# Sample tokens of a product-key expert layer by gathered rows, 384 dense tokens, and gate products in half steps

## The reference, cut to what matters

```python
q = (xb @ w_pq).reshape(..., 8 heads, 2, 128)
s = einsum('thpd,phnd->thpn', q, sub_keys)          # 128 keys per half
s1, i1 = top_k(s[:, :, 0], 16); s2, i2 = top_k(s[:, :, 1], 16)
top, pos = top_k(s1[..., :, None] + s2[..., None, :], 16)
eidx = (i1 * 128 + i2) at pos                       # 16 experts per head
gate = softmax(top)
a = einsum('thkd,td->thk', u_tab[eidx], xb)
out = einsum('thk,thkd->td', gelu(a) * gate, v_tab[eidx])
```

## Time and profile before

| | |
|---|---|
| median of 3 runs | 1866.88 us (1865.66 to 1868.56) |
| profiled execution | 1866.18 us |
| its span | 1864.5 us |
| TensorE busy | 1780.4 us (95%) |
| VectorE / ScalarE / GpSimd busy | 63% / 39% / 58% |
| DMA | 442.39 MB, mean 237 GB/s |
| mean granted TensorE clock | 0.978 |

### The profile page before, as it was taken

The page is one execution under the profiler, slowest core; times in us unless marked ns, Lnnn a source line. Parts: engine busy times, 40 slices in busy tenths (PEclk is TensorE's granted clock), DMA queues, the critical chain, the costliest instruction groups (busy, mean ns, idle before and its releaser), DMA issues.

```text
span 1864.5 us, 27254 instructions
## 1 busy us (share of the span) xinstructions
PE 1780.4 (95%) x10594; PEld 1698.5 (91%) x10594; DVE 1183.9 (63%) x2350; ACT 728.1 (39%) x983; POOL 1083.0 (58%) x612
## 2 busy tenths in 40 slices
PE   7899999799999999999999998999999999999995
PEld 3899887688999999999999998989999999999995
DVE  3441343627898799985666665446677777777746
ACT  2454232323333333354554544443444444444431
POOL 1667221132337788854554454477877888887851
PEclk9899999899999999999999999999999999999997
DMA  8545121233215888868687786799999999999951
GB/s 273 172 148 170 62 97 57 75 113 103 91 51 163 273 275 281 275 211 276 233 269 242 250 260 217 228 400 369 363 353 357 377 350 377 353 368 361 364 185 48
DMA packets 191200, 442.39 MB, mean 237 GB/s; under 512 B 20064, under 2 KB 106080, under 8 KB 190816
## 3 DMA queue, kind: packets, MB, share of 16 engines
q1 hardware_dynamic: 82320, 251.88, 39.5%
q0 software_dynamic: 36864, 134.23, 19.4%
q10 hardware_dynamic: 71888, 54.53, 8.8%
HBM read 381.42 MB, written 59.17 MB: 236 GB/s over the span
## 4 chain that ended last, share of the span: by engine, by line
PE 87%; DVE 4%; DMA 3%; ACTq 2%; ACT 2%; issue 1%; POOL 1%; SPq 0%; DVEq 0%; POOLq 0%
PE ps L866 57%; PE ps L652 17%; PE ps L876 5%; ACTq L1136 2%; PE ps L672 2%; PE ps L681 1%; DMA gelu_scratch<-ga 1%; PE ps L841 1%; ACT stage L1143 1%; DMA tab<-in_tab 1%; DMA raw<-in_w 1%; ACT tHi L1092 1%; PE ps L764 0%; DMA ug<-in_urows,eidx 0%; PE ps L798 0%
## 5 line engine op out<-in xcount | busy, mean ns | idle before, releaser
L612 POOL TENSOR_TENSOR tLo<-tab,tHi 128x1024 fp32r<-128x1024 f32 x256 | 635.5, 2482 | 357.9 <-ACT tHi L1092 356.5
L1092 ACT CAST tHi<-tab 128x1024 fp32r<-128x1024 f32 x256 | 267.9, 1047 | 331.9 <-PE ps L866 321.1
L866 PE MATMUL ps<-actHi,tLo 128*128 128x416 f32 x1024 | 361.7, 353 | 5.5 <-issue 5.3
L866 PE MATMUL ps<-hHi,tLo 128*128 128x416 f32 x1024 | 364.5, 356 | 0.0
L866 PE MATMUL ps<-hLo,tHi 128*128 128x416 f32 x1024 | 361.6, 353 | 0.0
L866 PE MATMUL ps<-actHi,tHi 128*128 128x416 f32 x1024 | 359.6, 351 | 0.0
L866 PE MATMUL ps<-hHi,tHi 128*128 128x416 f32 x1024 | 358.8, 350 | 0.0
L866 PE MATMUL ps<-actLo,tHi 128*128 128x416 f32 x1024 | 357.4, 349 | 0.0
L600 POOL TENSOR_TENSOR wLo<-raw,wHi 128x1024 fp32r<-128x1024 f32 x53 | 127.7, 2409 | 316.0 <-ACT wHi L930 316.0
L866 PEld LDWEIGHTS ps<-actHi,tLo 128*128 128x128 f32 x1024 | 192.5, 188 | 7.6 <-issue 5.6
L866 PEld LDWEIGHTS ps<-hHi,tHi 128*128 128x128 f32 x1024 | 193.2, 189 | 2.8
(11 more groups left out here) (310 smaller groups left out, 2617.8 us busy)
## 6 DMA issues: line engine op xcount, KB each, us to landing
tab<-in_tab SPq DMA_DIRECT2D x256, 512.0 KB, 6.1
raw<-in_w SPq DMA_DIRECT2D x101, 512.0 KB, 3.9
gelu_scratch<-ga ACTq DMA_DIRECT2D x128, 208.0 KB, 4.4
gate_scratch<-stage ACTq DMA_DIRECT2D x13, 2048.0 KB, 14.1
gt<-gate_scratch SPq DMA_DIRECT2D x32, 832.0 KB, 5.8
gin<-gelu_scratch SPq DMA_DIRECT2D x128, 208.0 KB, 7.8
xT<-in_xT SPq DMA_DIRECT2D x1, 2176.0 KB, 10.0
out_y<-yo SPq DMA_DIRECT2D x8, 272.0 KB
```

Source lines behind the costliest of these rows:

```text
L612: pool.tensor_tensor(tLo[:, n % SPL], tab[:, n % TABS], tHi[:, n % SPL].bitcast(F32), ALU.subtract).then_inc(s_tlo, 1)
L866: last = mm(ps[:, bank, 0:TD], w, x[:, k, 0:TD], start=first, stop=end)
L1092: nc.scalar.copy(tHi[:, n % SPL], tab[:, n % TABS]).then_inc(s_thi, 1)
```

## The change

- The dense tokens are now 384 prompt tokens (TD = 384); the sparse tile holds the last 128 prompt tokens.
- The 32 sample tokens also go by gathered rows: a partition holds one token and one of four groups of two heads, so their 4096 picks are 32 items (PB) ahead of the 128 others. Items are NDOT = 160 per table, 320 in all, in place of 256. ScalarE repeats their query and their h four times (`q_b`, `h_b`); they have a retrieval of their own with two heads, run first; h is brought to rows twice, after chunk 3 for the samples and after chunk N_SHUF = 51 for the prompt. The four partial sums are added by a product with a folded identity after chunk 168.
- Dots: eight in each of the four tiles of level two, tile 0 among them; two with each of 48 gate steps; 32 after them, three per chunk; so that all dots are done ahead of the second pass. Row sums follow at 10 in 7 chunks.
- Gate steps begin at chunk 52 over 64 chunks. The products of a step go in two halves, over three PSUM banks (4, 5, 7), with a wait and a copy for each half.
- Three gelu buffers in place of two, one semaphore each.
- The picks' transposes, of three tiles in place of four, stand at chunk 51, and the sum over the samples is read at chunk 168.

The core of the diff:

```diff
-TD = T - P
-STILES = [TD, 0, 128, 256, TD - P]
+TD = T - P - TS
+STILES = [TD, 0, 128, 256]
...
-NIT = 2 * P
-L2_DOTS = 10
-N_SHUF = 56
-G_FIRST, G_SPAN = 57, 60
-N_GELU = NCH + 20
+PB = P * TS // P
+NDOT = P + PB
+NIT = 2 * NDOT
+L2_DOTS = 8
+N_SHUF = 51
+G_FIRST, G_SPAN = 52, 64
+N_GELU = NCH + 2
+GATE_BANKS = (4, 5, 7)
...
-    due = NIT - 152 + min(152, (n - NCH + 1) * 13 // 10)
-    return due if n > N_GELU else min(due, P)
+    if n < NCH:
+        return min(NDOT, PB + 2 * NSTEP + 3 * (n - G_FIRST - G_SPAN))
+    return NDOT + max(0, min(NDOT, (n - N_GELU) * 10 // 7))
 
 
 def item_time(q):
 
-    if q < 40:
-        return 14 + q
-    if q < 92:
-        return G_FIRST + (q - 40) * G_SPAN // NSTEP
-    if q < 104:
-        return 120 + (q - 92) * 2 // 3
-    return NCH + (q - 104) * 10 // 13
+    if q < PB:
+        return 12 + q
+    if q < PB + 2 * NSTEP:
+        return G_FIRST + (q - PB) // 2 * G_SPAN // NSTEP
+    if q < NDOT:
+        return G_FIRST + G_SPAN + (q - PB - 2 * NSTEP) // 3
+    return N_GELU + (q - NDOT) * 7 // 10
 
...
-        ga = at("ga", [P, 2, TD], SPL_AT + 24576)
+        ga = [at(f"ga{i}", [P, TD], (SPL_AT + 24576, SPL_AT + 24576 + 4 * TD, pos_sq + 6528)[i]) for i in range(3)]
...
             def gather(q):
 
                 if q == 0:
-                    pool.wait_ge(s_eidx, 1)
+                    pool.wait_ge(s_hr, 1)
+                if q == 0 or q == PB:
+                    pool.wait_ge(s_eidx, 1 if q == 0 else 2)
                 if q >= UG:
                     pool.wait_ge(s_item, q - UG + 1)
-                pool.indirect_dma_start(ug[:, q % UG, :], None, a["urows"] if q < P else a["vrows"],
-                                        bass.IndirectOffsetOnAxis(ap=eidx[:, q % P:q % P + 1], axis=0)).then_inc(s_ug[q % UG], 16)
+                pool.indirect_dma_start(ug[:, q % UG, :], None, a["urows"] if q < NDOT else a["vrows"],
+                                        bass.IndirectOffsetOnAxis(ap=eidx[:, q % NDOT:q % NDOT + 1], axis=0)).then_inc(s_ug[q % UG], 16)
...
-                if st:
-                    pe.wait_ge(s_gev, st)
-                for t in range(STEP_TOK):
-                    out = ps[:, 4 + t // 4, t % 4 * P:(t % 4 + 1) * P]
-                    last = mm(out, oh2[:, st % 2, t, :], w1[:, st % 2, t, :], start=True, stop=True)
-                last.then_inc(s_gmm, 1)
+                for part in range(2):
+                    i = 2 * st + part
+                    if i >= len(GATE_BANKS):
+                        pe.wait_ge(s_gev, i - len(GATE_BANKS) + 1)
+                    for t in range(4):
+                        last = mm(ps[:, GATE_BANKS[i % 3], t * P:(t + 1) * P], oh2[:, st % 2, 4 * part + t, :],
+                                  w1[:, st % 2, 4 * part + t, :], start=True, stop=True)
+                    last.then_inc(s_gmm, 1)
 
...
+                if n == 3:
+                    pe.wait_ge(s_idr, 1)
+                    pe.wait_ge(s_hb, 1)
+                    sparse_h((h_b[:, 0], h_b[:, 1]))
...
+                    pe.wait_ge(s_item, PB)
+                    sparse_h((hHi[:, :, TD:TP], hLo[:, :, TD:TP]))
...
+                    for part in range(2):
+                        i, t0 = 2 * st + part, STEP_TOK * j + 4 * part
+                        act.wait_ge(s_gmm, i + 1)
+                        f(stage[:, b % 2, :, t0:t0 + 4].rearrange("p c t -> p t c"),
+                          ps[:, GATE_BANKS[i % 3], :].rearrange("p (t c) -> p t c", c=P), ACT.Identity).then_inc(s_gev, 1)
...
+            where = [best_b[:, 1], best_b[:, 2]]
+            retrieve(2, m16_b[:], ix_b[:], best_b[:, 0], where, lambda part: None)
+            indices(eidx[:, 0:PB], where)
+            for i in range(NST):
+                where = [best[:, 1, i, :], best[:, 2, i, :]]
+                retrieve(PH, m16[:, i], ix[:, i], best[:, 0, i, :], where, lambda part: sparse(L2_DOTS * i + part))
                 if i == 0:
-                    stt(eidx[:], best[:, 1, 0, :], float(NKEY), best[:, 2, 0, :], ALU.mult, ALU.add).then_inc(s_eidx, 1)
...
-                sparse(4 * L2_DOTS + st + 1)
+                sparse(PB + 2 * (st + 1))
...
-            sparse(4 * L2_DOTS + NSTEP + 4)
-            v.wait_ge(s_gev, NSTEP)
+            sparse(sparse_until(NCH - GRP))
+            v.wait_ge(s_gev, 2 * NSTEP)
             for c in range(GRP):
                 act_32(c)
-                sparse(4 * L2_DOTS + NSTEP + 5 + c)
                 act_lo(c)
+                sparse(sparse_until(NCH - GRP + c))
+            sparse(NDOT)
```

More of the change, by code:

```diff
@@ L418, in build @@
         s_gelu = sem("gelu_ready")
[L419 removed]
+        s_gas = [sem(f"gelu_stored{i}") for i in range(3)]
         s_oh = sem("one_hots_ready")
@@ L851, in _, with sparse_h @@
             key_scores(HP - 1)
[L853 to L857, removed]
+            def sparse_h(parts):
+                for k in range(KT):
+                    for i in range(2):
+                        last = mm(h_rows[:, k * P:(k + 1) * P], parts[i][:, k], identR[:], start=(i == 0), stop=(i == 1))
+                last.then_inc(s_hr, 1)
             def product(n, hi_in, lo_in, bank):
@@ new lines, in _, with retrieve @@
+                if j % 8 == 7:
+                    for u in (j // 8 * 2, j // 8 * 2 + 1):
+                        last = top16([m16_b[:, u]], [ix_b[:, u]], [sc_b[:, u, :]])
+            link(last)
+            def retrieve(nh, m, x, top, where, some):
+                nk = nh * PK
+                rank = iota[:, 0:PK].unsqueeze(1).broadcast_to([P, nk, PK])
+                cand_, tcur_, pos_, pab_ = cand[:, 0:nh], tcur[:, 0:nh], pos16[:, 0:nk], pab[:, 0:nk]
+                pabf_, pcut_, ixf_ = pabf[:, :, 0:nk], pcut[:, 0:nk], ixf[:, 0:2 * nh]
+                nc.vector.tensor_copy(ixf_, x)
+                halves = m.rearrange("p (h two) k -> p h two k", two=2)
+                half = ixf_.rearrange("p (h two) k -> p h two k", two=2)
+                tt(cand_[:, :, 0:16], halves[:, :, 0, 0:1].broadcast_to([P, nh, PK]), halves[:, :, 1, :], ALU.add)
+                link(tt(cand_[:, :, 16:RAGGED].rearrange("p h (a b) -> p h a b", b=8), over(halves[:, :, 0, 1:PK], 8),
+                        halves[:, :, 1, 0:8].unsqueeze(2).broadcast_to([P, nh, PK - 1, 8]), ALU.add))
+                some(1)
+                for h in range(nh):
@@ L1520, in _ @@
[L1520 to L1524 removed]
+                some(5)
+                tt(top.rearrange("p (h k) -> p h k", k=PK), tcur_, over(tcur_[:, :, 0], PK),
+                   ALU.subtract).then_inc(s_top, 1)
+                link(tsc(pab_, pos_, 8.0, 8.0, ALU.max, ALU.subtract))
@@ new lines, in retrieve @@
+                for w, e in enumerate(both):
+                    last = tt(e.rearrange("p h k a -> p (h k) a"), rank, over(pabf_[:, w], PK), ALU.is_equal)
+                link(last)
+                for w, e in enumerate(both):
+                    last = tt(e, e, half[:, :, w, :].unsqueeze(2).broadcast_to([P, nh, PK, PK]), ALU.mult)
+                link(last)
+                some(7)
+                for w, e in enumerate(both):
+                    last = nc.vector.tensor_reduce(where[w], e.rearrange("p h k a -> p (h k) a"), AXX, ALU.add)
@@ new lines, in retrieve, with indices @@
+                link(last)
+            def indices(out, where):
+                stt(out, where[0], float(NKEY), where[1], ALU.mult, ALU.add).then_inc(s_eidx, 1)
+            for g in range(P // TS):
+                nc.vector.tensor_copy(fold[TS * g:TS * (g + 1), :], ident[TS * g:TS * (g + 1), TS * g:TS * (g + 1)])
+            where = [best_b[:, 1], best_b[:, 2]]
[4 more added lines that the diff above has]
+                retrieve(PH, m16[:, i], ix[:, i], best[:, 0, i, :], where, lambda part: sparse(L2_DOTS * i + part))
```

231 lines of the change are left out of this document (123 added, 108 removed).

## The result

The changed kernel takes 1854.73 us (median, 1851.93 to 1856.32) against 1866.27 us: ratio 0.9937, 95% interval 0.9921 to 0.9953. It is 0.6% faster, 12 us and not the 72 that were forecast, and lies outside the range of 1766 to 1832. The profiled execution took 1855.86 us, 61.9 more than the 1794.0 of the sum.

The account below looks back on a forecast made before the run. TensorE, busy 95% of the span with matmuls in a row, was taken as the bound. Terms -83.6 - 7.1 + 3.0 + 13 - 12.5 + 11 + 4 = -72.2 took 1866.2 to 1794 us, range 1766 to 1832.

Parts of the forecast that it names:

- chunk of the first pass, x128: First pass: with 384 columns for 416, a chunk of products takes 4.205 us, down from 4.535.
- retrieval, stalls and clock: First pass up to the picks: late gather buffers 10 us plus 3 us for the lower clock, +13 (0 to +22).
- P(0): Start of chunk 0's product (P(n) is the start of chunk n's), taken as 546.2 us.
- second pass above 128 x 4.18: Second pass: TensorE's pace of 4.18 us a chunk holds; 4 us (0 to +25) added for fold and lack of slack.
- Between the passes: Chunks 115 to 128: 32 row sets gathered, three a chunk, make TensorE wait 16 us for 5.3, +11 (0 to +25).
- Gate stage: Gate steps: blocked issue B about 7 us, stall B - 5.2, eight times; 18 us with clock for 30.5, 12.5 less.
- rival D: Products: the 128-column weight load sets a floor of 187 ns or more, so fewer columns give nothing: 1877 us; chance 0.02.
- rival A: Second pass: transfers bound it at 363 GB/s, 4.59 us a chunk, and 9 us more between the passes: 1845 us; chance 0.10.
- C: Retrieval, gate stage and between the passes: all three waits at their upper ends, 1825 to 1835 us; chance 0.17.
- B: Whole kernel: buffers cover it; retrieval costs 3, gate stalls nearly go, second pass loses nothing: 1767 us; chance 0.15.

## Why the prediction was wrong

Against 1855.86 us, the terms of the sum that moved, in us (P(n) and G from the timelines):

| step | predicted | measured | difference |
|---|---|---|---|
| stalls between the passes (end of chunk 115 to P(128)) | 16 | 79 | +63 |
| stalls of the gate stage | 18 | 28.5 | +10.5 |
| chunk of the first pass, x128 | 4.205 | 4.2175 | +1.6 |
| retrieval, stalls and clock | 13 | about 5 | -8 |
| P(0) | 546.2 | 545.1 | -1.1 |
| second pass above 128 x 4.18 | 8.6 | 7.6 | -1 |

They add to +65; 3 us less are spread over the rest.

**The step that failed is "Between the passes".** It put 11 to 13 us down twice, once by counting GpSimd's work and once by bytes, and took 16. Work and bytes are sums, and neither sees a wait that goes in a circle. I had followed the ring of six gather buffers item by item in the retrieval, where it cost about 4 us, and not here, where each gather behind the split of chunk n needs a dot that VectorE has been given for chunk n, behind the low part that needs the product of chunk n. With six buffers and three dots a chunk, the ring reaches back two chunks; the gathers are issued one chunk ahead of their time and the dots asked for one chunk behind it, and nothing is left. In the kernel before, 12 row sets stood here, not 32. The loop is shown by three runs: opened on VectorE by two chunks it gives 49 us back, by one chunk 44, opened on GpSimd 40. The clock adds to it, since TensorE idles 10 us a turn: the granted clock is 0.70 in that stretch and a product takes 6.36 to 6.80 us, against 4.22.

Of the 79 us, the loop is 49. A second part begins after the last gate block: the issue of the gelu store was blocked for 17.16 us, where the last of the kernel before took 4.92, and TensorE stood 9.94 us. With the loop opened, the chain goes on through three waits of 11 to 13 us for gathered rows. Halves or quarters of the store did little for this part, fewer gathers did (H 54.7). The rows of before had no such mix, and I had charged it at the few microseconds of a late row; no single run takes it apart.

**Gate stage.** The formula (a stall of B - 5.2 for a blocked issue B, eight times) was right in kind. It gives 4.7, 3.9, 1.8 and 3.9 us for the issues of 9.88, 9.14, 6.95 and 9.14 us, and TensorE waited 4.67, 3.93, 1.77 and 3.93. Behind 9.79 and 10.75 it waited 1.77 and 2.73, a chunk later. These six are all the waits above 0.2 us, 18.8 in sum; that the mean B of 8.9 times eight gives 30, near the 28.5 of the whole stage, is luck. Less gathered traffic or halves, with B at 5.7 or less in the mean, leave about 1 us in the whole stage. What was wrong is B, taken as "about 7" from gathers passing at 410 GB/s. With twice as many gathers it rose by 2.8 us and not by 1.3. The other 9.7 us of the 28.5 are nearly all work that ran longer at a lower clock, where the term had 4. The mean granted clock of 0.98 hides it, and the five microseconds behind the longest wait show it (stretch as above):

```profile
819.00:824.00 5.00, 4.47 (x17) 4.47 (x18) 2.35 (x2) 4.53 (x6) 2.33 (x1) 0.50 0.71 244
```

**What was right.** Products take 174.3 and 175.7 ns, as 13.6 ns a matmul less had it, so rival D (weight loads) is out. The first dot came at 595.24 after 21.81 us, said was 596.5 and 24; the picks were ready at 771, said was 770, and the stall at chunks 40 to 42 was there at under half its price (4.2 us for 10, which went with the paced gathers). Its rows in the changed kernel, VectorE and then GpSimd:

```profile
595.24 1.22 DVE L1476 SCALAR_TENSOR_TENSOR ug<-ug,ps 128x1024 f32<-128x1024 f32 x1 [21.81 <-DMA ug<-in_urows,eidx]
```

```profile
716.52 0.95 POOL L640 DMA_INDIRECT ug<-in_urows,eidx  x1 [5.89 <-DVE ug L1476]
...
722.17 0.96 POOL L640 DMA_INDIRECT ug<-in_urows,eidx  x1 [2.33 <-DVE ug L1476]
```

The second pass runs at TensorE's pace, 318.2 us busy of 320 at 391 GB/s: rival A is refuted. By the limit of 358 GB/s that the Trainium skill gives (DMA: Bandwidth & Descriptors, Specifications) this could not be; the trace disagrees. The Trainium skill also says (HBM Reference, Specifications (TRN2)) that a core streaming alone gets well above that share, about 425, and the 391 here and the 410 of the earlier trace rows agree with it.

**The rivals.** C, supply chains that pile up, named the right kind but stopped at 20 us for this stretch, since it was built from the same sums. That my range ended at 1832 is the same omission: no case held a wait that feeds itself. B's 1767 took it that the buffers cover all; that needed smaller stores.

## What to carry to other kernels

Where a change lets an engine wait for a ring of buffers, write down for one late item what it waits for, what that stands behind on its own engine, and go on until the trail leaves the chunk or comes back to it. If it comes back, the period is the sum of all latencies of the turn over the number of chunks that it spans, whatever the busy times and the bytes say; here moving one list by one chunk was worth 44 us. And an engine that both computes on the critical path and issues large stores of short rows is best given them in pieces no longer to drain than its consumers can do without it.

## Not expected of the hardware

- An issue on ScalarE's queue behind a 2 MB store of 4096 short rows was blocked for 4.6 to 7.8 us with one gather a step beside it (the kernel before), 6.4 to 10.8 with two and 17.2 with three a chunk (the changed kernel). Behind stores of 512 KB it was never over 2.1 with the gathers spread, and up to 7.0 with three a chunk.
- A DMA share of 1.01 at 362 GB/s stood beside a TensorE that never waited for 346 us (gathers spread, stores in quarters). The share says that the engines always have something to do, not that anyone is late.
